# Masked attention by pairs of heads, with the values stationary and the probabilities divided before they are turned

## The reference, cut to what matters

```python
# first block, even mixer: 8 heads, queries and keys of 96, values of 64, causal
# second block, twice: 8 sparse heads with one common key and value head, 8 forgetting heads with their own
logits = jnp.einsum("bqhd,bqkd->bqhk", qb, k_sel).astype(jnp.float32) * att_scale      # sparse
logits = jnp.einsum("bqhd,bshd->bhqs", qb, k).astype(jnp.float32) * scale              # forgetting
logits = logits + jnp.moveaxis(cq, 1, 2)[..., None] - cum_k[:, :, None, :]
p = jax.nn.softmax(logits, axis=-1).astype(v.dtype)
out = jnp.einsum("bhqs,bshd->bqhd", p, v)
```

## Time and profile before

| | |
|---|---|
| median of three runs | 3442.46 us |
| the profiled execution's own time | 3443.18 us |
| its span in the trace | 3441.5 us |
| PE busy | 3358.2 us, 98% |
| DVE busy | 1790.0 us, 52% |
| ACT busy | 1471.7 us, 43% |
| POOL busy | 1433.9 us, 42% |
| granted clock of PE, mean | 0.997 |

### The profile page before, as it was taken

One profiled execution on the slowest core, in us unless ns is written; L12 is line 12 of the kernel. 1 busy time (PEld: TensorE's weight loads), 2 busy tenths in 40 slices (PEclk: granted clock), 3 DMA queues, 4 the chain that ended last, 5 costly groups with the idle time before them and its releaser, 6 DMA issues. The chain is left out here.

```text
span 3441.5 us, 49476 instructions
## 1 busy us (share of the span) xinstructions
PE 3358.2 (98%) x19319; PEld 2796.6 (81%) x19319; DVE 1790.0 (52%) x3313; ACT 1471.7 (43%) x2970; POOL 1433.9 (42%) x1268
## 2 busy tenths in 40 slices
PE   8999999999999899999999999999999999999999
PEld 7778778888877687888888878888888878888887
DVE  4655574636456674565463286455153186445243
ACT  4672354323344554532333347344343246544343
POOL 3320154454443545444544431345554432345543
PEclk9999999999999999999999999999999999999999
DMA  4210024545321122344443220222323220123321
GB/s 117 78 44 15 27 86 135 196 147 170 99 89 50 36 88 88 111 149 168 159 147 111 84 74 14 74 86 92 104 83 101 91 79 26 50 86 98 98 92 56
DMA packets 232836, 317.89 MB, mean 92 GB/s; under 512 B 9909, under 2 KB 149148, under 8 KB 232604
## 3 DMA queue, kind: packets, MB, share of 16 engines
q1 hardware_dynamic: 203206, 261.55, 23.6%
q10 hardware_dynamic: 29398, 53.17, 4.6%
HBM read 312.59 MB, written 2.10 MB: 91 GB/s over the span
## 5 line engine op out<-in xcount | busy, mean ns | idle before, releaser
L364 PE MATMUL banks<-split,split 128*128 128x512 f32 (+2 forms) x11760 | 2681.0, 389 | 24.2 <-ACT split L383 13.6
L364 PEld LDWEIGHTS banks<-split,split 128*128 128x128 f32 x11760 | 2185.3, 188 | 496.3 <-ACT split L383 24.5
L387 POOL TENSOR_TENSOR split<-kept,split 128x512 fp32r<-128x512 f32 (+2 forms) x1158 | 1356.8, 1176 | 1709.9 <-ACT split L383 1707.2
L383 ACT ACTIVATE split<-kept 128x512 fp32r<-128x512 f32 (+2 forms) x1158 | 646.3, 564 | 1454.3 <-PE banks L364 1408.0
L1590 DVE SCALAR_TENSOR_TENSOR work<-banks,kept,work 128x511 f32<-128x511 f32 (+1 forms) x176 | 120.5, 746 | 257.0 <-ACT work L1572 256.2
L910 DVE SCALAR_TENSOR_TENSOR work<-work,kept 128x512 f32<-128x512 f32 x168 | 194.5, 1158 | 6.0
L855 DVE SCALAR_TENSOR_TENSOR kept<-banks,kept 128x512 f32<-128x512 f32 x48 | 33.3, 746 | 209.6 <-PE banks L364 209.6
L853 DVE TENSOR_TENSOR kept<-banks,kept 128x512 f32<-128x512 f32 x64 | 40.6, 685 | 195.2 <-PE banks L364 195.2
L540 DVE COPY work<-banks 128x512 f32<-128x512 f32 (+1 forms) x64 | 37.4, 644 | 195.4 <-PE banks L364 195.3
L1165 PE MATMUL banks<-work 128*128 128x128 f32 x928 | 136.4, 277 | 1.0 <-ACT work L1241 0.6
L1165 PEld LDWEIGHTS banks<-work 128*128 128x128 f32 x928 | 118.6, 192 | 6.0 <-ACT work L1241 2.8
(11 more groups left out here) (413 smaller groups left out, 3079.8 us busy)
## 6 DMA issues: line engine op xcount, KB each, us to landing
work<-in_mod_w ACTq DMA_DIRECT2D x48, 1024.0 KB, 6.0
kept<-in_ffn_w SPq DMA_DIRECT2D x94, 512.0 KB, 4.8
kept<-in_w_up SPq DMA_DIRECT2D x88, 512.0 KB, 4.8
kept<-in_w_in SPq DMA_DIRECT2D x36, 1024.0 KB, 5.0
kept<-in_od_w_in SPq DMA_DIRECT2D x20, 1024.0 KB, 5.1
kept<-in_ffn_w SPq DMA_DIRECT2D x18, 1024.0 KB, 5.4
kept<-in_w_down SPq DMA_DIRECT2D x18, 1024.0 KB, 4.9
kept<-in_ev_w_in SPq DMA_DIRECT2D x8, 1024.0 KB, 5.1
```

What stands on the lines that cost most here:

```text
L364: m = pe.matmul(self.bank(q, j), lhs, rhs, start=t == 0 and i == 0, stop=t == job.KT - 1 and i == 2)
L383: act.activation(self.weights(s, 0), self.source(s), ACT.Copy).then_inc(self.rounded, 1)
L387: pool.tensor_tensor(self.weights(s, 1), self.source(s), self.weights(s, 0), ALU.subtract).then_inc(self.k.slices_split, 1)
```

## The change

`PairedHeads` takes the place of `Attend` in the first block's even mixer and is the new base of `StackedHeads`.

- Units go by pairs of heads: `place(u)` gives head `u // 8 * 2 + u % 2` and tile `u % 8 // 2`, so two heads take turns tile by tile.
- The reciprocal is taken as before by DVE, but now POOL multiplies the probabilities by it in place (`divide`) before PE transposes them; DVE no longer scales an output, and the probabilities have four tiles instead of two plus two.
- In `mix`, the values (128x64) are the stationary operand and the transposed probabilities the moving one; the two heads of a pair write partitions 0 to 63 and 64 to 127 of one bank, alternating. The result is already turned: `turn_o` is gone. A mix is done for two units at once, every second step.
- The copy of the turned probabilities is ACT's for t = 0 and 1 (`take_p`), DVE's for t = 2 and 3 (`move_p`).
- Scores run three units ahead instead of two. Queries (and new keys) of the next two heads are turned at steps 1 and 4 of 8 (`TURN`; 1 and 3 in the even mixer), their laying twice on POOL stands at steps 0 and 3, 1 and 4.
- At the start, two heads are turned instead of one; in the gate stage POOL lays three tiles twice (queries 0, keys 0, queries 1). Head 1 uses bank 6, keys 1 of the even mixer bank 7.
- There are more tiles for turned queries (four; three in the even mixer) and keys (five pairs; three).
- Where `memT` lies is rounded up to eight words.

The core of the diff (the removed methods of the old `StackedHeads` that only moved are left out):

```diff
-class StackedHeads(Attend):
+class PairedHeads:
+
+    QB, KB, SB, TB, OB = 2, 3, (6, 7), (0, 1), (4, 5)
+    AHEAD = 3
+    SECOND_Q, SECOND_K = 6, 7
+    TURN = (1, 3)
...
+    def place(self, u):
+
+        return u // 8 * 2 + u % 2, u % 8 // 2
...
+    def by_scalar(self, u):
+        return self.place(u)[1] < 2
...
+    def coming(self, u, steps):
+
+        h = u // 8 * 2 + 2
+        return [h + i for i in range(2) if h + i < len(self.heads) and steps[i] == u % 8]
...
+    def await_scores(self, pe, u):
+        h, t = self.place(u)
+        if t == 0:
+            pe.wait_ge(self.q_ready, max(h, 1) + 1)
+            pe.wait_ge(self.k_ready, self.heads[h].keys + 1)
+        if u >= 2:
+            pe.wait_ge(self.peaked, u - 1)
...
+    def turn_p(self, pe, u):
+        pe.wait_ge(self.scaled, u + 1)
...
+        for c in range(self.place(u)[1] + 1):
+            m = pe.transpose(self.bank(self.TB[u % 2])[:, c * P:(c + 1) * P], self.prob[u % 4][:, c * P:(c + 1) * P],
+                             self.k.ident)
+        m.then_inc(self.p_turned, 1)
+
+    def mix(self, pe, m):
+
+        u = 2 * m
+        h, t = self.place(u)
+        if self.by_scalar(u):
+            pe.wait_ge(self.p_taken, self.count_taken(u + 1))
+        else:
+            pe.wait_ge(self.p_moved, self.count_moved(u + 1))
+        if t == 0 and h >= 4:
+            pe.wait_ge(self.o_ready, h // 2 - 1)
+        for c in range(t + 1):
+            for i in range(2):
+                ins = pe.matmul(self.o_bank(h // 2)[i * 64:i * 64 + 64, t * P:(t + 1) * P], self.heads[h + i].v(c),
+                                self.probT[(u + i) % 4][:, c * P:(c + 1) * P], start=c == 0, stop=c == t)
+        ins.then_inc(self.mixed, 1)
...
+    def go_on(self, pe):
+        for u in range(self.AHEAD):
+            self.scores(pe, u)
+        for u in range(self.units):
+            for h in self.coming(u, self.TURN):
+                self.turn_q(pe, h)
+                if self.new_keys(h):
+                    self.turn_k(pe, h)
+            if u + self.AHEAD < self.units:
+                self.scores(pe, u + self.AHEAD)
+            self.turn_p(pe, u)
+            if u % 2 == 0 and u:
+                self.mix(pe, u // 2 - 1)
+        self.mix(pe, self.units // 2 - 1)
+        self.k.keep_busy(pe, self.TB[0], 6)
...
+    def go_on_scalar(self, act):
+        for u in range(self.AHEAD - 1):
+            self.exps(act, u)
+        for u in range(self.units):
+            if u + self.AHEAD - 1 < self.units:
+                self.exps(act, u + self.AHEAD - 1)
+            for h in self.coming(u, self.TURN):
+                self.take_q(act, h)
+                if self.new_keys(h):
+                    self.take_k(act, h)
+            if self.by_scalar(u):
+                self.take_p(act, u)
+            if u % 8 == 1 and u > 8:
+                self.round_o(act, u // 8 - 1)
+        self.round_o(act, self.units // 8 - 1)
...
+    def vector(self, dve, _link, q, c):
+        self.begin_vector(dve)
...
+        for u in range(self.units):
+            if u + self.AHEAD < self.units:
+                self.peak(dve, u + self.AHEAD)
+            if u + self.AHEAD - 1 < self.units:
+                self.invert(dve, u + self.AHEAD - 1)
+            for h in self.coming(u, self.TURN):
+                self.rest_q(dve, h)
+                if self.new_keys(h):
+                    self.rest_k(dve, h)
+            if not self.by_scalar(u):
+                self.move_p(dve, u)
+            if u % 8 == 2 and u > 8:
+                self.rest_o(dve, u // 8 - 1)
+            self.aside_vector(dve, u)
...
+    def divide(self, pool, u):
+        tile = self.prob[u % 4][:, 0:self.width(u)]
+        pool.wait_ge(self.inverted, u + 1)
+        pool.tensor_scalar(tile, tile, self.inv[:, u % 8:u % 8 + 1], None, ALU.mult).then_inc(self.scaled, 1)
...
+class StackedHeads(PairedHeads):
+
+    ASIDE = 12
+    TURN = (1, 4)
+    STAGE_Q, STAGE_K = (0, 3), (1, 4)
...
     def begin_pool(self, pool):
         self.stage_q(pool, 0)
         self.stage_k(pool, 0)
+        self.stage_q(pool, 1)
 
     def pool(self, pool):
-        for h in range(1, len(self.heads)):
-            self.stage_q(pool, h)
-            if self.new_keys(h):
-                self.stage_k(pool, h)
+        for u in range(self.units):
+            for h in self.coming(u, self.STAGE_Q):
+                self.stage_q(pool, h)
+            for h in self.coming(u, self.STAGE_K):
+                if self.new_keys(h):
+                    self.stage_k(pool, h)
+            self.divide(pool, u)
...
-    attend = Attend(k, heads, QK ** -0.5, W(48), o_hi, o_lo, QK, V_MLA, lambda t: t + 1, ready, masked=True, idle_first=14)
+    tiles = [k.view(W(n), S) for n in range(46, 60)]
+    attend = PairedHeads(k, heads, QK ** -0.5, tiles[0:3], tiles[3:6], tiles[6:10], tiles[10:14], W(60), o_hi, o_lo, QK, ready,
+                         idle_first=14)
```

More of the change, by code:

```diff
@@ new lines, in turn_q, with turn_k @@
+    def turn_q(self, pe, h):
+        if h >= 2:
+            pe.wait_ge(self.q_ready, h)
+        for t in range(ST):
+            m = pe.transpose(self.q_bank(h)[:, t * P:(t + 1) * P], self.heads[h].q[:, t, :], self.k.ident)
+        m.then_inc(self.q_turned, 1)
+    def turn_k(self, pe, h):
+        if self.heads[h].keys >= 2:
+            pe.wait_ge(self.k_ready, self.heads[h].keys)
+        for t in range(ST):
+            m = pe.transpose(self.k_bank(self.heads[h].keys)[:, t * P:(t + 1) * P], self.heads[h].k[:, t, :], self.k.ident)
+        m.then_inc(self.k_turned, 1)
@@ new lines, in await_scores, with scores @@
+    def await_scores(self, pe, u):
[5 more added lines that the diff above has]
+            pe.wait_ge(self.peaked, u - 1)
+    def scores(self, pe, u):
+        h, t = self.place(u)
+        n = self.width(u)
+        self.await_scores(pe, u)
+        pe.matmul(self.bank(self.SB[u % 2])[:, 0:n], self.q_tile(h)[0:self.dk, t * P:(t + 1) * P],
+                  self.k_tile(self.heads[h].keys)[0:self.dk, 0:n], start=True, stop=True).then_inc(self.scored, 1)
@@ new lines, in rest_q, with rest_k, peak @@
+    def rest_q(self, dve, h):
+        pass
+    def rest_k(self, dve, h):
+        pass
+    def peak(self, dve, u):
+        h, t = self.place(u)
+        n = self.width(u)
+        dve.wait_ge(self.scored, u + 1)
+        if u >= 4:
+            dve.wait_ge(self.p_turned, u - 3)
+        dve.tensor_tensor_reduce(self.prob[u % 4][:, 0:n], self.bank(self.SB[u % 2])[:, 0:n], self.heads[h].mask(t), 1.0, -NEG,
+                                 ALU.add, ALU.min, self.top[:, u % 8:u % 8 + 1]).then_inc(self.peaked, 1)
@@ L1409, in turn_k @@
         m.then_inc(self.k_turned, 1)
[L1411 to L1414, removed]
     def scores(self, pe, u):
[L1417 to L1426, removed]
+        h, t = self.place(u)
+        head, n = self.heads[h], self.width(u)
+        self.await_scores(pe, u)
+        if head.forget and t == 0:
+            pe.wait_ge(head.forget.done, 1)
+        bank, q = self.bank(self.SB[u % 2])[:, 0:n], self.q_tile(h)[:, t * P:(t + 1) * P]
+        high, low = self.k_tile(head.keys)
+        pe.matmul(bank, q, high[:, 0:n], start=True, stop=False)
         if head.forget:
@@ L1453, in take_k, with take_p @@
         act.wait_ge(self.k_turned, keys + 1)
[L1454 to L1464, removed]
+        self.await_k_tile(act, keys)
+        act.activation(self.k_tile(keys)[0], self.k_bank(keys), ACT.Copy).then_inc(self.k_rounded, 1)
+    def take_p(self, act, u):
+        super().take_p(act, u)
+        if u == self.ASIDE + 4:
+            self.aside.round(act)
     def rest_k(self, dve, h):
```

212 lines of the change are left out of this document (175 added, 37 removed).

## The result

The changed kernel takes 3454.94 us (median of 5 runs, 3451.97 to 3461.83) against 3442.46: a ratio of 1.0041 (95% interval 1.0028 to 1.0054). It is slower by 0.4%; I had forecast 3434 and a range up to 3446. The profiled execution took 3459.71 us, its span is 3458.0.

A forecast was written before the change was run, and what follows sets the result against it. PE's own stream was taken to bound the attention stages. Second stages -7.1 us, first stage -2.3, gate stages +1.0 sum to -8.4, from 3442.46 to 3434 us; own range 3427 to 3441, full range 3414 to 3446.

The forecast's parts named there:

- The form's drain: On PE, going into and out of half-array work for each mix costs 0.35 us, +1.4 a pair.
- PE's stream: PE's work per pair in the attention stages, without waits: forgetting 11.9 us, sparse 9.75, first stage 11.9.
- The end of the second stage: After the last full pairs (13.1 each): half a pair, 5.2 us, to the last score, then 9.25.
- PE's wait at the gate stage's start: GpSimd lays a third tile twice there, so PE's wait of 1.04 us should read 1.6.
- the division's price: GpSimd's division of 512 keys, between a copy (0.62 us) and a two-input operation (1.35), taken as 0.9.
- Case (d): Rival: GpSimd's division, if later than 1.8 us for 512, stops P(6) and P(7); left in (c)'s share, together 0.11.
- a walk of a forgetting pair: Late steps followed across engines: PE waits 1.07 and 0.45 us for VectorE's moves, +1.2 a pair after drain overlap.
- at the full granted clock: PE ran at full clock in the attention stages before; a granted clock leaving 1.00 would show the forecast wrong.
- the signs of being wrong: Waits naming GpSimd's division, second stages changing by different amounts, the clock leaving 1.00, time between stages moving.
- (a): Rival: VectorE doesn't hold the mixes, PE's stream alone counts; 19 us less, 3415; chance 0.22.
- (b): Rival: handovers at moves and mix switches cost 0.1 more each; 8 us more, 3442, no change; chance 0.12.
- (c): Rival: VectorE's queue in steps 4 to 6 delays moves, 0.8 us a pair; 3450; chance 0.11 including the late division.

The follow-up runs named there:

- the fastest version: Changed kernel with VectorE dividing 512-key tiles, ScalarE copying 384-key tiles, and each mix a step later, old order kept: 3421.07 us, 0.9939 of the kernel before.
- the cheap division: Changed kernel with GpSimd dividing only the first 128 columns of each probability tile, 0.60 us for every width: 3456.39 us, 1.0035 of the kernel before.
- ScalarE's copies and the late mix: Changed kernel with ScalarE copying the 384-key tiles and each mix one step later, GpSimd still dividing every tile: 3446.86 us, 1.0012 of the kernel before.
- products in the waits: Changed kernel with idle products in each stage's fill and before the division waits of steps 5, 6 and 7: 3460.03 us, 1.0051 of the kernel before.

## Why the prediction was wrong

**What held.** The 800 mix records are there, the output's transposes are gone. The form's drain: three transposes start 0.48 ahead of a mix (0.33 without one) and its 8 records end 0.58 later (0.44), 0.29 in all, 0.36 around a mix of 12; the forecast had 0.35. The Trainium skill's page "TensorEngine Tiling (Array Packing)", section "Key Properties", says that changing the tiling mode drains TensorE; the rows agree, at 0.29 to 0.36 us a mix. PE's stream was no longer than I had it: in the fastest version a sparse pair takes 9.89 (9.75 without waits in the forecast), and a forgetting pair 12.12 with a wait of 0.81 in it (11.9 without waits). A steady forgetting pair takes 13.20 (forecast 13.1). The end of the second stage, from the last pair but one on, takes 26.45 (27.55). PE's wait at the gate stage's start reads 1.73 (1.6).

**The step that failed first: the division's price.** I bounded it by 0.62 and 1.35 for 512 keys and took 0.9; it is 1.56, outside my bounds. The divisions of a pair take 8.7 us of GpSimd's time, where I had "at most 7.4"; it is busy for 80.8 of 108.7 us. The Trainium skill's "GPSIMD Engine Reference", section 3.1, has 0.77 for 512 elements of a tight loop, half of what this case measures; the measurement decides. I chose the copy as the nearest row because it reads one tensor; the row of the two-input operation was the nearer one, and still too low. The four forms give 283 ns + 2.5 ns an element. This step alone does not carry the miss: with the division at 0.60 for every width, under my 0.9, the second block's stages still take 106.6 where I had 99.3. The next two steps failed with it.

**The step on when it would be late.** Case (d) let it be late only from 1.8 us on, and 1.56 was late. That bound stood on a walk of a forgetting pair alone. In the sparse pair shown, 2 us shorter on PE, the waits ahead of P(4), P(5) and P(6) name the division at 1.24 and 1.56 us; that pair takes 13.82, 3.4 of it at half clock. The sparse pair before it, at the full clock, waits for the division for 0.46 ahead of P(6) and 0.24 ahead of P(8) and takes 11.51, forecast 10.65; a first-stage pair takes 13.34, forecast 12.4. The walk also left out the chain exponential 6, queries' copy, their rest, score 9 (0.7 of a wait in a forgetting pair of the changed kernel, up to 1.4 in the one with the cheap division).

**The step "at the full granted clock".** I priced PE's waits at their length. Behind them the clock fell, three times within the first four pairs of the second stage and twice in its repetition. The same pair with a different time at half clock, in the two repetitions: 13.16 with 6.8 us and 12.14 with 3.4; 14.67 with 6.8 and 13.82 with 3.4; 14.33 with 3.4 and 13.03 without. That is 0.25 to 0.38 us a us at half clock, not 0.5, since a part lies in waits. Two runs of the cheap division, 3444.44 at a mean clock of 0.995 and 3458.20 at 0.990, say 0.40 (0.005 of 3450 is 34.5 us at half clock). A line through all repeated runs of the changed kernel and its fifteen variants, time against mean clock, each kernel about its own mean, gives 0.37; it is an estimate, as the clock is on record to 0.001. The changed kernel's 0.994 against 0.997 is then worth some 8 of its 12.5 us over the kernel before; at the old clock it would be near 3447, still slower than forecast by 13.

**The sum.** The forecast in terms of the profiled execution is 3434.8; it took 3459.7. The stages are 5.1, 9.4 and 7.8 over forecast, the rest 2.8 (two more stretches of 3.4 at half clock are in it, at 22.0, ahead of all that is changed, and at 2858.5, in the gate stage). Of the 22.2 in the stages, 27.3 us at half clock are worth 7 to 11; 11 to 15 are waits for the division and the chain above. All the signs of being wrong that I had named came: the waits name GpSimd's division, the clock leaves 1.00, the two second stages change by different amounts (5.8 and 4.2), and the time outside the stages grows by 3.8 where I had 1.0.

**The rivals.** (a), PE's stream alone at 3415, needed the waits to be gone, which they were not; with two edits the kernel comes near it (3421). (b), dearer handovers, has little room beside it: a sparse pair of that version is 0.14 over my stream. (c) was nearest by its number (3450). It had the place, VectorE's queue, but not the main cause: taking the 384-key copies off that queue gives 4 us, which the intervals hardly tell from none, and the moves of 512 keys wait (2.6 us in a second stage) for transposes, most of which wait for GpSimd. (d), the late division, which I put at nothing at the two-input price, is what happened at 1.56. What is left open: how much of the fastest version's 6.6 us of idle time a second stage could lose, why the clock fell further with the cheap division, and the clock's price inside a stage apart from the waits, since no run held the clock there without adding work.

## What to carry to other kernels

An operation that moves onto a slow engine inside a loop of handovers is priced by its own form, not by a copy's: if no row has it, take the dearest neighbour as the least it may cost and ask in the *shortest* iteration when it becomes late. Where two waits stand one behind the other, removing one shows little (1 and 11 us here) and removing both shows far more than the sum (34): try them together before dropping one. Read the mean clock of every run beside its time: here it hid a gain of some 8 us. And an idle time of PE can cost more than its length: add some 0.3 to 0.4 us for every us that the record of the clock then shows at half.

## What was not expected of the hardware

- GpSimd's multiplication by a scalar for each partition takes 603, 923, 1243 and 1563 ns for 128x128 to 128x512 in fp32, more than its operations on two tensors of 512 (1117 to 1355 ns in other rows of the profile after); VectorE takes 477 to 486 for 512.
- PE at 89% busy in a stage, with no single idle time over 1.2 us, is granted half the clock for up to 13.7 of 109 us. The second stage with ScalarE's copies and the late mix, where PE is busy for 87.59 of 100.28 us, is granted 1.00 all through.
- Runs of one kernel spread more where the clock falls: 9.9 us for the changed kernel, 1.5 us for the one with products in the waits, all of whose runs had 0.997.
